# First mixer: the last output unit gets weight places of its own and six of its row blocks go ahead of the last heads' rows

## What is computed

```python
def attn_pool_mixer(h, ...):
    proj = h @ w_in
    q, k, v, u = jnp.split(proj, ...)
    ...
    o = diff_attention(q[:, :, 0], q[:, :, 1], k[:, :, 0], k[:, :, 1], v, lam)
    o = rmsnorm(o, subln_g) * (1 - lam_init)
    ...
    p = multiscale_pool(u, pool_w, pool_scale)
    return jnp.concatenate([o, p], axis=-1) @ w_out
```

## Time and profile before

| what | value |
|---|---|
| median of 3 runs | 1503.95 us (1502.12 to 1504.21) |
| profiled execution, its own time | 1502.93 us |
| its span in the trace | 1501.1 us |
| PE busy | 94% of the span |
| DVE busy | 60% |
| ACT busy | 41% |
| granted PE clock, mean over the span | 0.975 of full speed |

### The profile page before, as it was taken

The page is one execution under the profiler, slowest core; times in us unless marked ns, Lnnn a source line. Parts: engine busy times, 40 slices in busy tenths (PEclk is TensorE's granted clock), DMA queues, the critical chain, the costliest instruction groups (busy, mean ns, idle before and its releaser), DMA issues.

```text
span 1501.1 us, 26991 instructions
## 1 busy us (share of the span) xinstructions
PE 1410.7 (94%) x11552; PEld 1263.5 (84%) x11552; DVE 898.0 (60%) x1044; ACT 619.5 (41%) x740; POOL 19.1 (1%) x24
## 2 busy tenths in 40 slices
PE   7999999989999999999999999999999989995666
PEld 5999999989999989999999999999997989762223
DVE  4877775657877768777776655556557644420002
ACT  3534345555434453443444544445434643420002
POOL 0000000400000000000000000000000000000000
PEclk9999999999999999999999999999999999998779
DMA  9998867516988758788655465553635439999996
GB/s 363 323 328 300 287 251 246 152 54 245 322 302 303 258 190 313 281 299 305 206 169 169 135 209 189 175 188 123 196 96 177 158 138 350 378 420 421 420 421 271
DMA packets 204056, 380.34 MB, mean 253 GB/s; under 512 B 12741, under 2 KB 158154, under 8 KB 192202
## 3 DMA queue, kind: packets, MB, share of 16 engines
q1 hardware_dynamic: 203616, 379.08, 70.3%
q10 hardware_dynamic: 362, 0.14, 0.0%
HBM read 378.14 MB, written 1.05 MB: 253 GB/s over the span
## 4 chain that ended last, share of the span: by engine, by line
PE 82%; DMA 9%; DVE 4%; ACT 3%; issue 2%; SPq 1%; DVEq 0%; ACTq 0%
PE ps L697 18%; PE ps L699 17%; PE ps L698 17%; PE ps L725 11%; PE ps L726 5%; DMA plain_whi<-in_w_exp_down_dram 4%; PE ps L1486 2%; ACT whi L1599 2%; DMA raw<-in_w_exp_down_dram 2%; DVE wlo L2051 1%; DMA spare<-in_w_exp_down_dram 1%; DMA plain_whi<-in_w_ada_dram 1%; PE ps L1460 1%; PE ps L1444 1%; PE ps L815 1%
## 5 line engine op out<-in xcount | busy, mean ns | idle before, releaser
L2051 DVE TENSOR_TENSOR wlo<-raw,whi 128x2048 fp32r<-128x2048 f32 (+2 forms) x187 | 423.1, 2263 | 226.8 <-ACT whi L1599 226.7
L1599 ACT ACTIVATE whi<-raw 128x2048 fp32r<-128x2048 f32 (+2 forms) x187 | 352.7, 1886 | 153.6 <-PE ps L699 138.0
L697 PE MATMUL ps<-h_both,whi 128*128 128x256 f32 x1320 | 380.1, 288 | 1.0 <-DVE wlo L2051 0.9
L699 PE MATMUL ps<-h_both,wlo 128*128 128x256 f32 x1320 | 374.5, 284 | 0.0
L698 PE MATMUL ps<-h_both,whi 128*128 128x256 f32 x1320 | 374.4, 284 | 0.0
L697 PEld LDWEIGHTS ps<-h_both,whi 128*128 128x128 f32 x1320 | 251.3, 190 | 8.7 <-issue 4.1
L725 PE MATMUL ps<-h_both,whi 128*128 128x512 f32 x704 | 252.3, 401 | 0.0
L698 PEld LDWEIGHTS ps<-h_both,whi 128*128 128x128 f32 x1320 | 251.5, 191 | 0.7 <-issue 0.5
L699 PEld LDWEIGHTS ps<-h_both,wlo 128*128 128x128 f32 x1320 | 251.5, 191 | 0.0
L697 PE MATMUL ps<-hidhi,whi 128*128 128x256 f32 x704 | 201.3, 286 | 2.1 <-DVE wlo L2214 2.1
L699 PE MATMUL ps<-hidhi,wlo 128*128 128x256 f32 x704 | 199.4, 283 | 0.0
(11 more groups left out here) (352 smaller groups left out, 1867.7 us busy)
## 6 DMA issues: line engine op xcount, KB each, us to landing
ada_raw<-in_w_ada_dram SPq DMA_DIRECT2D x66, 1024.0 KB, 5.3
raw<-in_ffn_wg_dram SPq DMA_DIRECT2D x44, 1024.0 KB, 6.8
raw<-in_ffn_wu_dram SPq DMA_DIRECT2D x44, 1024.0 KB, 5.4
raw<-in_ffn_wd_dram SPq DMA_DIRECT2D x44, 1024.0 KB, 6.4
raw<-in_w_in_dram SPq DMA_DIRECT2D x18, 1024.0 KB, 5.3
raw<-in_w_in_c_dram SPq DMA_DIRECT2D x12, 1024.0 KB, 5.3
raw<-in_w_in_ab_dram SPq DMA_DIRECT2D x8, 1024.0 KB, 8.6
raw<-in_w_exp_down_dram SPq DMA_DIRECT2D x7, 1024.0 KB, 16.7
```

What stands on the lines that cost most here:

```text
L697: pe.matmul(o, wh, xh, start=start, stop=False, skip_group_check=shared)
L699: return pe.matmul(o, wl, xh, start=False, stop=stop, skip_group_check=shared)
L1599: act.activation(whi[s][:, 0:width], raw[s][:, 0:width], ACT.Copy).then_inc(high[s], 1)
L2051: dve.tensor_tensor(wlo[s][:, 0:width], raw[s][:, 0:width], whi[s][:, 0:width].bitcast(F32), ALU.subtract).then_inc(split[s], 1)
```

## The change

Unit 11's high and low parts get two tiles of their own, `apart_hi` and `apart_lo`, laid over `spare0` and `spare1`. ACT writes the high part behind `probsT_of(3)` and DVE the low part behind unit 10's refill; the refills of slot 2 in ACT's `norm` and in DVE's `add_units` (j = 0) are taken out. PE runs the row blocks 4 to 7, 0 and 1 of unit 11 behind those of unit 10, and its row blocks 2 and 3 last, behind those of units 8, 9 and 10.

```diff
+        apart_hi = sb_over("apart_hi", "spare0", 0, [P, UW])
+        apart_lo = sb_over("apart_lo", "spare1", 0, [P, UW])
...
-            def output_part(s, b, k, xh, xl, last=False):
+            def output_part(s, b, k, xh, xl, last=False, apart=False):
...
-                    mm = three(ps[:, b, m * T:(m + 1) * T], whi[s][:, c], wlo[s][:, c], xh[:, k, :], xl[:, k, :],
-                               False, last, shared=True)
+                    mm = three(ps[:, b, m * T:(m + 1) * T], (apart_hi if apart else whi[s])[:, c], (apart_lo if apart else wlo[s])[:, c],
+                               xh[:, k, :], xl[:, k, :], False, last, shared=True)
...
-                    output_part(s, b, k, mhi, mlo, last and k == ks[-1])
+                    output_part(s, b, k, mhi, mlo, last and k == ks[-1], apart=(u == 11))
...
             out_rows(10, (0, 1))
-            for u in (8, 9, 10):
+            out_rows(11, (4, 5, 6, 7), first_=True)
+            out_rows(11, (0, 1))
+            for u in (8, 9, 10, 11):
                 out_rows(u, (2, 3), last=True)
-            linear("mix0", 11, "x_ready", mhi, mlo, b=out_bank[11])
...
-                    if pr < len(slots):
+                    if pr < len(slots) and slots[pr] is not None:
                         refill(slots[pr])
...
             probsT_of(3)
+            act.wait_ge(landed[2], (turn[2] + 1) * 16)
+            act.activation(apart_hi[:, :], raw[2][:, :], ACT.Copy).then_inc(high[2], 1)
+            turn[2] += 1
             o_out(1)
             column_roots(36, 4, P)
             o_high(1)
-            norm((2, 0, 1))
+            norm((None, 0, 1))
...
-                    if j < 3:
+                    if j < 3 and (stage, j) != ("mix0", 0):
                         refill(s)
...
             refill(1)
+            dve.wait_ge(high[2], turn[2] + 1)
+            dve.tensor_tensor(apart_lo[:, :], raw[2][:, :], apart_hi[:, :].bitcast(F32), ALU.subtract).then_inc(split[2], 1)
+            turn[2] += 1
             column_inverse(36, 4)
```

## The result

| | kernel before | changed kernel |
|---|---|---|
| median of 7 runs each | 1503.48 us (1501.48 to 1504.63) | 1510.08 us (1505.68 to 1511.01) |
| ratio | 1 | 1.0035, 95% interval 1.0026 to 1.0044 |
| profiled execution | 1502.93 us, span 1501.1 | 1507.04 us, span 1505.2 |

The change loses 5.3 us by the ratio, which is that of the means (1508.6 to 1503.3). The changed kernel's executions fall into two groups: with five more from the first experiment they are 1505.7, 1506.0 and 1507.0 at a mean granted clock of 0.974 to 0.976, and nine between 1509.7 and 1512.1 at 0.969 to 0.972. The forecast was slower, at 1507.3 with a range to 1509.0; the median lies above that range, and which of its terms was too small is the subject of the experiments.

A forecast was written before the change was run, and what follows sets the result against it. TensorE held 82% of the chain, but DVE reached the mixer's end almost together with it. A later last addition (2.05) plus a fallen clock (1.3) gave +3.35 us on 1503.95, so 1507.3; 8-in-10 range 1503.8 to 1509.0.

The forecast's parts named there:

- PE is through earlier: End of the first mixer: two PE idle stretches of 2.63 us go, opening a bank costs 0.48, so 2.15 us earlier.
- Unit 11's split and its load cost nothing: Mixer: early rounding, remainder and load fall where ACT and DVE idle, with some 2.8 us of cover; no cost.
- The last addition comes 2.05 us later: Mixer's end on DVE: last addition to x, behind both ffn1 splits, ends 2.05 us later, plus or minus 0.3.
- The clock falls in PE's gap: Ahead of the norm: two idle stretches of some 2.4 and 2.6 us lower PE's clock; 1.3 us, between 0 and 1.7.
- the argument against a second low stretch: Norm ahead of ffn1: PE runs the norm's own filling matmuls before asking for its result; a second stretch would make 3.4 us.
- Rival (c): Low clock lasts two stretches, or a later stage falls into one: near +5 us, 1508.9; chance 0.13.
- rival (a): Mixer's end: same late addition, clock kept at full: +2.05 us, 1506.0; chance 0.17.
- Rival (b): Mixer's end: not slower, DVE no bound, mixer ends with PE 2.15 us earlier; 1501.8; chance 0.08.

The follow-up runs named there:

- the first experiment: The changed kernel run again unedited, beside the kernel before, for a second profile: 1510.41 us, ratio 1.0047.
- places alone: Against the kernel before, only unit 11's own places and early split; PE's order as before, no bank opened: 1501.10 us, ratio 0.9985.
- additions-first version: Changed kernel with DVE's four additions ahead of its two ffn1 splits, PE and ACT unchanged: 1504.48 us, ratio 1.0011 to the kernel before.
- two-block version: Changed kernel with two of unit 11's row blocks ahead of the last heads' rows instead of six: 1503.09 us, ratio 1.0004 to the kernel before.
- late addition: Kernel before with one DVE memset put ahead of the last addition to x, nothing of the change in: 1508.93 us, ratio 1.0031.
- the second comparison: The unedited changed kernel measured again against the kernel before: 1510.41 us, ratio 1.0047.
- the filled version: Changed kernel with 20 zero matmuls on PE ahead of the sums of units 10 and 11 each: 1505.60 us, ratio 1.0015 to the kernel before.
- the second gap filled: Changed kernel with 20 zero matmuls on PE only ahead of the last sums: 1507.49 us, ratio 1.0021 to the kernel before.

## Why the prediction was right in direction and too small in size

- **PE is through earlier.** Forecast 2.15 us plus or minus 0.1; measured some 2.5 against the mlo row: the opening and each matmul were a little shorter than the rows of before had them. It gained nothing, as forecast.
- **Unit 11's split and its load cost nothing.** Right: places alone contains both and is 2.3 us faster than before.
- **The last addition comes 2.05 us later.** Right: 14.71 - 12.88 = 1.83 from the mlo on, and 0.08 ahead of it (from the copy of the probabilities at 315.11 to the mlo 10.16 us, before 10.08), together 1.9. Filling PE's gaps leaves just this, +1.9 in the trace and +2.2 in the time. The reason given, DVE's program order with two ffn1 splits ahead of the last addition, is what the additions-first version removes and the two-block version shortens by the number of blocks.
- **The clock falls in PE's gap.** Right as a mechanism, which filling the gaps takes away and a late addition alone brings. **The size is the step that failed**: 1.3 us forecast, 14.95 - 11.54 = 3.4 and 15.61 - 11.54 = 4.1 measured. The forecast priced it by the matmuls lost at 306 to 310 and took off what would pass idle. But the low stretch there lasted under 4 us, here 10 and 13.7; the norm's zero matmuls, named as the argument against a second low stretch, did not end it in either profile, and they and the sixteen openers, at half speed, held up ffn1's first rows by themselves (PE's first matmul there starts at 349.03, 3.2 us behind DVE's first product of the norm at 345.86; before 345.77 and 344.08, 1.7 us). A gap can cost what was forecast: that of the two-block version cost 1.25 us. Why the clock came back after 3.4 us there, and in the changed kernel only after 10 or more, no run shows.
- **The sum.** 1.9 + 3.4 to 4.1 = 5.3 to 6.0 us, against 5.3 by the ratio and 7.0 between the medians of the second comparison. (The second profile also reaches the mlo row 1.2 us later than that of before, 328.12 against 326.88, with a low clock at 287 to 290.5 that the profiles of before and of the first changed run do not have.) Rival (c), given 0.13, was nearest with 1508.9; rival (a), clock kept at full, is what the filled version shows with its 1505.6. Rival (b), PE as the bound, is excluded by DVE's rows.
- The profiled execution of the changed kernel is only 4.1 us above that of before. It is 0.6 us ahead at the pool's mlo (304.19 against 304.78) and wins 1.1 more up to the next copy of the probabilities (4.88 against 5.99 us), where its clock held; so it comes to the last heads' mlo 1.6 us early, loses 5.2 from there to the eviction, and 0.5 behind it. That its 1507.04 lies next to the forecast's 1507.3 is luck.

The Trainium skill ("TensorE: Matmul & The Clock Gate", section on the HAM clock gate) advises not to fit the ramp to a count, since it is small beside a typical kernel's span, and says that its phase is not fixed from run to run. The traces agree with both: 3.4 to 4.1 us are under 0.3% of the span, and the low stretch lasted 10.2 us in one profile of the changed kernel and 13.7 in the other. But beside a loss of 5.3 us the clock was the larger part, so here it could not be left out.

## What to carry to other kernels

Work put ahead on the engine that waits is only worth what the next engine in the chain can take: count that engine's queue up to the hand-over, in program order, and from the row that starts it, before moving anything in front of that row. Where a change makes TensorE finish early, look at how long it will then stand idle, take the whole stretch until dense work runs again as what the clock may cost (gaps of about one length cost 1.25 us in one version here and 3.4 to 4.1 in another), and fill the gap or leave it closed. Take a change of two halves apart: here one half alone was 0.15% faster, and the whole 0.35% slower.

## What the runs showed of the hardware that was not expected

- A low clock can last. In the changed kernel's profiles PE ran at the lower level for some 10.2 and 13.7 us, although from 342 us on in the one and 344.4 in the other it was busy without a break, with the norm's last sums, 8 zero matmuls, the spread, 16 more zero matmuls and ffn1's first rows; in the kernel before the 8 and the 16 took 1.21 and 1.98 us at the full clock, against 2.08 and 3.65. In two other profiles the stretch was over after about 3.4 us: with the second gap filled, where 20 zero matmuls follow the gap that cost the clock, and with two blocks ahead, where nothing is filled.
- Idle stretches of 2.4 to 2.6 us ahead of the last sums were enough, with the mixer's dense row blocks and 48 short sums right before them: 2.38 us in the two-block version, 2.62 in the kernel before with the late addition; 0.8 to 1.0 us never showed it here. One and the same wait can go either way: PE waits 1.64 to 1.65 us for the pool's mlo near 304 us in the eleven profiles in which that wait is not filled; the clock fell behind it in nine and held in two (the changed kernel's first, and additions first).
- Single executions of one kernel differ by up to 8 us (additions first) with the mean granted clock, so a comparison of such kernels needs several executions and the clock of each.
